# Picks spread over the first PEER product, dots through a ring of three, and POOL making the lower part of U for one quarter in four

## The reference

```python
q = (xb @ w_q).reshape(T, PEER_HEADS, 2, PEER_QDIM // 2)
s = jnp.einsum('thpc,hpkc->thpk', q, sub_keys)
top_s, top_i = lax.top_k(s, PEER_TOPK)
cand = top_s[:, :, 0, :, None] + top_s[:, :, 1, None, :]
best_s, best_c = lax.top_k(cand.reshape(T, PEER_HEADS, PEER_TOPK * PEER_TOPK), PEER_TOPK)
ids = i1 * N_KEYS + i2            # i1, i2 from top_i by best_c
g = jax.nn.softmax(best_s, axis=-1)
act = jax.nn.gelu(jnp.einsum('td,thkd->thk', xb, u_tab[ids]), approximate=False)
w = (g * act).astype(xb.dtype)
out = jnp.einsum('thk,thkd->td', w, v_tab[ids])
```

## Time and profile before

| what | us |
|---|---|
| median of three runs | 2987.31 |
| lowest, highest | 2981.48, 2988.35 |
| the profiled execution's own time | 2983.09 |
| its span | 2981.3 |
| PE busy | 2801.1 (94%) |
| DVE busy | 2345.2 (79%) |
| POOL busy | 1576.7 (53%) |
| ACT busy | 969.3 (33%) |
| first matmul of quarter 0, last quarter's start | 753, 1480.6 |

### The profile page before, as it was taken

How to read it: one execution, slowest core, us unless ns; L and a number is a source line. 1 busy time by engine, 2 the same in 40 slices (tenths; PEclk the granted TensorE clock), 3 DMA queues, 4 the chain that set the end, 5 groups by cost and what they waited for, 6 DMA issues and landing times.

```text
span 2981.3 us, 33747 instructions
## 1 busy us (share of the span) xinstructions
PE 2801.1 (94%) x12016; PEld 2151.1 (72%) x12016; DVE 2345.2 (79%) x3821; ACT 969.3 (33%) x1331; POOL 1576.7 (53%) x1235
## 2 busy tenths in 40 slices
PE   7999689999688899999979999999999999999998
PEld 3546544788567688888767777777777777777776
DVE  2787943587999977777568888888888888888886
ACT  2014232311144466666222323223223223232233
POOL 1999400011011265666157777777777777777640
PEclk9999589999899999999989999999999999999999
DMA  3111010212335599999998888889888888898883
GB/s 121 39 46 54 3 43 0 78 43 78 130 121 170 162 332 366 366 362 362 351 339 304 301 305 317 296 301 317 301 303 310 300 306 308 298 320 288 317 290 142
DMA packets 253976, 685.16 MB, mean 230 GB/s; under 512 B 31984, under 2 KB 97648, under 8 KB 248432
## 3 DMA queue, kind: packets, MB, share of 16 engines
q0 software_dynamic: 104448, 335.81, 32.4%
q1 hardware_dynamic: 83568, 313.65, 28.6%
q10 hardware_dynamic: 65792, 33.56, 3.9%
HBM read 611.60 MB, written 71.30 MB: 229 GB/s over the span
## 4 chain that ended last, share of the span: by engine, by line
PE 66%; DVE 24%; DVEq 3%; issue 2%; DMA 2%; ACT 2%; another core or an unknown queue 1%; SPq 0%; ACTq 0%
PE ps L1604 21%; PE ps L1596 14%; PE ps L1569 11%; PE ps L1527 6%; DVE ps L1214 6%; DVE hnT L895 4%; PE ps L1455 3%; PE ps L1555 3%; PE ps L1364 2%; DVE ul L1187 2%; DVE wl L1284 1%; PE ps L1324 1%; DMA u_raw<-in_uT 1%; DVE lx L1061 1%; PE ps L1419 1%
## 5 line engine op out<-in xcount | busy, mean ns | idle before, releaser
L523 POOL DMA_INDIRECT vring<-in_v_tab,idsA x512 | 547.3, 1069 | 323.9 <-DVE ps L1214 193.9
L1214 DVE SCALAR_TENSOR_TENSOR ps<-vring,hsel,ps 128x1024 f32<-128x1024 f32 x508 | 652.0, 1283 | 15.3 <-DVE ps L1214 0.5
L512 POOL DMA_INDIRECT hsel<-hidden,idsE x384 | 436.8, 1138 | 159.8 <-issue 109.0
L1604 PE MATMUL ps<-vh,wh 128*128 128x512 f32 x1024 | 403.8, 394 | 28.4 <-DVE wl L1284 28.4
L1596 PE MATMUL ps<-xh,uh 128*128 128x512 f32 x1024 | 408.3, 399 | 12.0 <-DVE ul L1187 11.4
L1604 PE MATMUL ps<-vh,wl 128*128 128x512 f32 x1024 | 405.7, 396 | 0.0
L1596 PE MATMUL ps<-xh,ul 128*128 128x512 f32 x1024 | 405.1, 396 | 0.0
L1604 PE MATMUL ps<-vl,wh 128*128 128x512 f32 x1024 | 403.6, 394 | 0.0
L1596 PE MATMUL ps<-xl,uh 128*128 128x512 f32 x1024 | 402.7, 393 | 0.0
L1569 PE MATMUL ps<-hx,xh 128*128 128x512 f32 x768 | 314.5, 410 | 52.9 <-DVE lx L1061 51.6
L498 POOL TENSOR_TENSOR hot<-marks,selG 128x1024 f32<-128x1024 bf16 x64 | 140.1, 2190 | 364.6 <-PE ps L1555 227.0
(11 more groups left out here) (187 smaller groups left out, 4960.7 us busy)
## 6 DMA issues: line engine op xcount, KB each, us to landing
xraw<-in_uX SPq DMA_DIRECT2D x128, 512.0 KB, 6.5
u_raw<-in_uT SPq DMA_DIRECT2D x128, 512.0 KB, 7.3
v_raw<-in_v_tab SPq DMA_DIRECT2D x128, 512.0 KB, 5.4
gates<-gbuf ACTq DMA_DIRECT2D x16, 2048.0 KB, 23.7
gt<-gates SPq DMA_DIRECT2D x32, 1024.0 KB, 7.6
hidden<-hst SPq DMA_DIRECT2D x96, 256.0 KB, 8.1
wqbuf<-in_w_q SPq DMA_DIRECT2D x16, 512.0 KB, 3.4
vring<-in_v_tab,idsA POOLq DMA_INDIRECT x512, 5.8
```

The lines of the kernel that those rows point to most:

```text
L512: nc.gpsimd.indirect_dma_start(out=hsel[:, n, k:k + 1], out_offset=None, in_=hidden_items, in_offset=bass.IndirectOffsetOnAxis(ap=idsE[:, ...
L523: nc.gpsimd.indirect_dma_start(out=vring[r % VS][:, :], out_offset=None, in_=v_rows if r >= P else u_rows, in_offset=bass.IndirectOffsetOn ...
L1214: nc.vector.scalar_tensor_tensor(out=bank2(6), in0=vring[slot][:, :], scalar=w, in1=bank2(6), op0=ALU.mult, op1=ALU.add).then_inc(cb_done, 1)
L1604: last = mm(ps[:, 2 + k % 4, :], w[:, c, tt * P:(tt + 1) * P], v[:, c, dh * 512:(dh + 1) * 512], start=c == 0 and w is wh and v is vh, sto ...
```

## The change

- **Picks.** Five tiles (0, 4, 5, 6, 7; 70 steps) are done by quarter 36; the other three (42 steps) are spread over quarters 36 to 121.
- **Hot blocks** lie at quarters 21 + 1.5 n, the last at 115. The reload of x stays behind block 29.
- **Dots** lie in quarters 41 to 126, in a ring of three buffers (`vring` 2, 4 and 6), with semaphores of their own (`u_got`, `dot_read`); normed x is made at quarter 40. A gather waits for the dot three before. The eight `vring` gathers of V start after the last dot. Other buffers (`cand2`, `best`, `idf` and others) move so that the three are free while picks go on.
- **Lower part of U.** For quarters 6, 10, 14, ... (Q % 4 == 2, 31 of them) POOL makes `lx`, counting `lxp_ready`; DVE makes the others. PE and SP wait for the one or the other.
- **Last block.** Its sums go to `hlast`, not `hst`; SP loads the first gates before the stores of the last block; the reload of rows waits for `hlast`'s stores.
- **exps** (ACT's exponent for a tile) comes one quarter later in ACT's order.

```diff
-PICK_QUARTERS = 44
-X_BLOCK = PICK_QUARTERS // QB - 1
-X_QUARTER = PICK_QUARTERS + 4
+FIRST_PICKS = 1 + HT
+FIRST_QUARTERS = 36
+LAST_PICK = QUARTERS - 6
+X_BLOCK = FIRST_QUARTERS // QB - 1
+X_QUARTER = FIRST_QUARTERS + 4
 DOT_FROM = X_QUARTER + 1
+DOT_SLOTS = (2, 4, 6)
+US = len(DOT_SLOTS)
...
-def picks_done(qb):
-    return min(NT * STEPS_PICK, NT * STEPS_PICK * (qb + 1) // PICK_QUARTERS)
+def picks_done(Q):
+    first = FIRST_PICKS * STEPS_PICK
+    if Q < FIRST_QUARTERS:
+        return first * (Q + 1) // FIRST_QUARTERS
+    return min(NT * STEPS_PICK, first + (NT * STEPS_PICK - first) * (Q + 1 - FIRST_QUARTERS) // (LAST_PICK - FIRST_QUARTERS))
...
+def low_by_pool(Q):
+    return Q >= QB and Q % QB == 2
+
+def lows(Q, pool):
+    return sum(low_by_pool(q) == pool for q in range(Q + 1))
+
+def stores(slot):
+    return len(range(slot, (NB - 1) * PT, HSLOTS))
...
 def hot_quarter(n):
-    return 16 + n * 3 // 2
+    return 21 + n * 3 // 2
...
+def dots_done(Q):
+    return min(P, share(P, QUARTERS - 1 - DOT_FROM, max(0, Q + 1 - DOT_FROM)))
...
+        uring = [vring[k] for k in DOT_SLOTS]
+        hlast = at(0, "hlast", [P, PT, WIDTH])
...
+        def low_done(engine, Q):
+            engine.wait_ge(lxp_ready if low_by_pool(Q) else lx_ready, lows(Q, low_by_pool(Q)))
...
             def load_x(Q):
                 if Q >= QB:
-                    sp.wait_ge(lx_ready, Q - QB + 1)
+                    low_done(sp, Q - QB)
...
                 if B == NB - 1:
                     for c in range(2):
-                        sp.wait_ge(lx_ready, QUARTERS - QB + c + 1)
+                        low_done(sp, QUARTERS - QB + c)
                         sp.dma_start(u_raw[:, c, :], uT[c]).then_inc(u_in[c], 16)
+                    for slot in range(HSLOTS):
+                        sp.wait_ge(hst_out[slot], 16 * stores(slot))
+                    load_gates(0)
                 store_hidden(B)
-                if B == hot_quarter(HT * BLOCKS - 1) // QB + 2:
+                if B == hot_quarter(HT * BLOCKS - 1) // QB + 1:
...
+            def gather_dot(k):
+                if k == 0:
+                    pool.wait_ge(ids_ready, 1)
+                    pool.wait_ge(sel_ready, FIRST_PICKS)
+                elif k >= US:
+                    pool.wait_ge(dot_read, k - US + 1)
+                else:
+                    pool.wait_ge(xt_ready, 1)
+                nc.gpsimd.indirect_dma_start(
+                    out=uring[k % US][:, :], out_offset=None, in_=u_rows,
+                    in_offset=bass.IndirectOffsetOnAxis(ap=idsA[:, 0, k:k + 1], axis=0)).then_inc(u_got[k % US], 16)
...
             for Q in range(QUARTERS):
+                if low_by_pool(Q):
+                    pool.wait_ge(hx_ready, Q + 1)
+                    r = Q % QB
+                    nc.gpsimd.tensor_tensor(lx[r][:, :, :], xraw[:, r, :, :], hx[r][:, :, :].bitcast(F32),
+                                            ALU.subtract).then_inc(lxp_ready, 1)
                 for n in range(HT * BLOCKS):
                     if hot_quarter(n) - 1 == Q:
                         scale_hot(n)
...
+                for k in range(P):
+                    if quarter_of_dot(k) - 2 == Q:
+                        gather_dot(k)
...
-                if e >= HSLOTS:
+                if B < NB - 1 and e >= HSLOTS:
                     act.wait_ge(hst_out[e % HSLOTS], 16 * (e // HSLOTS))
-                nc.scalar.copy(hst[:, e % HSLOTS, :], ps[:, e % HSLOTS, :]).then_inc(h1_free, 1)
+                dst = hlast[:, n, :] if B == NB - 1 else hst[:, e % HSLOTS, :]
+                nc.scalar.copy(dst, ps[:, e % HSLOTS, :]).then_inc(h1_free, 1)
...
-                if Q >= QB:
+                if Q >= QB and not low_by_pool(Q):
                     low_wide(Q)
...
             def hidden_quarter(Q):
                 B, quarter = divmod(Q, QB)
-                pe.wait_ge(lx_ready, Q + 1)
+                low_done(pe, Q)
```

More of the change, by code:

```diff
@@ L126, in hot_quarter, with quarter_of_dot @@
 def hot_quarter(n):
-    return 16 + n * 3 // 2
[L130 to L135, removed]
+    return 21 + n * 3 // 2
+def dots_done(Q):
+    return min(P, share(P, QUARTERS - 1 - DOT_FROM, max(0, Q + 1 - DOT_FROM)))
+def quarter_of_dot(k):
+    return next(Q for Q in range(QUARTERS) if dots_done(Q) > k)
 def row_of_step(step):
@@ L314, in decoder_block @@
         el_in = [sem(f"el_in{k}") for k in range(VALUES_IN)]
-        xt_in, xt_ready, dot_done = sems("xt_in xt_ready dot_done")
+        xt_in, xt_ready, dot_read, dot_done, hlast_out = sems("xt_in xt_ready dot_read dot_done hlast_out")
+        u_got = [sem(f"u_got{k}") for k in range(US)]
         act_ready, wA_ready = sems("act_ready wA_ready")
@@ L380, in store_hidden @@
                     sp.wait_ge(h1_free, e + 1)
-                    sp.dma_start(hidden[n * P:(n + 1) * P, B * WIDTH:(B + 1) * WIDTH],
-                                 hst[:, e % HSLOTS, :]).then_inc(hst_out[e % HSLOTS], 16)
+                    dst = hidden[n * P:(n + 1) * P, B * WIDTH:(B + 1) * WIDTH]
+                    if B == NB - 1:
+                        sp.dma_start(dst, hlast[:, n, :]).then_inc(hlast_out, 16)
+                    else:
+                        sp.dma_start(dst, hst[:, e % HSLOTS, :]).then_inc(hst_out[e % HSLOTS], 16)
             load_wq(0)
@@ L440, in load_group @@
                     sp.dma_start(v_raw[:, c % VR, :], v_tab[g * GC + c]).then_inc(v_in[c], 16)
[L441 to L446, removed]
+                    if c == 1 and not first:
+                        sp.wait_ge(w_ready, g * GC)
                         load_gates(g)
             for c in range(VR):
-                sp.wait_ge(lx_ready, QUARTERS - VR + c + 1)
+                low_done(sp, QUARTERS - VR + c)
             load_group(0, first=True)
@@ L533, in _ @@
                         scale_hot(n)
[L534 to L542, removed]
+                for k in range(P):
+                    if quarter_of_dot(k) - 2 == Q:
+                        gather_dot(k)
+            rows = 0
             values = P
@@ L1202, in combine @@
                     dve.wait_ge(wA_ready, q // PER_GROUP + 1)
[L1203 to L1204 removed]
+                slot = q % VS
+                dve.wait_ge(v_got[slot], 16 * (q // VS + 1))
                 w = hsel[:, n, k:k + 1]
@@ L1222, in normed_rows @@
                 dve.wait_ge(selT_ready, HT)
-                nc.vector.scalar_tensor_tensor(out=bank2(6), in0=vring[6][:, :], scalar=small[:, 40:41], in1=vring[7][:, :],
+                nc.vector.scalar_tensor_tensor(out=bank2(6), in0=uring[1][:, :], scalar=small[:, 40:41], in1=uring[2][:, :],
                                                op0=ALU.mult, op1=ALU.mult).then_inc(xt_ready, 1)
@@ L1254, in _ @@
                     marked += 1
-                for r in range(items_done(Q - 1) if Q else 0, items_done(Q)):
-                    if r < P:
-                        dot(r)
-                    else:
-                        combine(r - P)
+                for k in range(dots_done(Q - 1) if Q else 0, dots_done(Q)):
+                    dot(k)
             for c in range(2):
```

71 lines of the change are left out of this document (37 added, 34 removed).

## The result

| what | us |
|---|---|
| median of the changed kernel, five runs (lowest, highest) | 2967.77 (2964.76, 2973.15) |
| the kernel before beside it on the same chip | 2981.68 (2980.73, 2988.35) |
| ratio, 95% interval | 0.9947 (0.993 to 0.9964) |
| profiled execution's own time, span | 2964.76, 2963.0 |

The change is faster by 14 us. I forecast 45 less: the direction was right, the size three times too large. The time came out nearest to that of the rival of a ring that binds moderately (2963).

What follows compares the result with a forecast made beforehand. DVE with the picks was taken as the bound until they end, then PE. Quarter 127 starting 43 us earlier and 2 us at the turn to the second product, off 2983.1, gave 2938, stated as 2940; range 2922 to 2978.

Steps and rivals of the forecast that it cites:

- the rival of a ring that binds moderately: Dots' ring: a gather of 8.5 us makes a turn of 11.4, quarter 127 starts at 1461, about 2963; chance 0.19.
- The first 36 quarters: Quarters 0 to 36, set by DVE's picks: quarter 36 starts at about 949 us, a gain of 51 us from there.
- Both hold, DVE narrowly: Quarters 36 to 127: DVE needs 4.8 to 5.1 us and POOL 3.8 per quarter of 5.35, both under PE.
- The ring of three: Dots on three buffers: a turn of 10.8 us, gather 7.9 of it; 42.7 turns take 461 us, ending at 1433.
- a dead heat: Dots' ring from quarter 41: a turn of 10.8 us equals PE's own pace of 10.8 us for three dots.
- The eight lows were nearly neutral: First 36 quarters: each lower part of U made by POOL takes 1.2 us from DVE, gives back 0.85 as interference.
- The rival that priced the lows at 2.4 each: POOL's lower parts of U cost DVE 2.4 us each, 12 us more in the first part; about 2960, chance 0.08.
- The last quarter: End of the first product: last gates store taken as 35 us; quarter 127 starts at 1438 against 1480.6, 43 us earlier.
- the turn to the second product: After quarter 127: DVE's 1.48 us wait for gt goes and two loads leave 1 to 2 us earlier, 2 us gained.
- the later counts and not the sum: Start of quarter 127: the store's 1432 lies beside the ring's 1433, so the later sets it, at 1435.
- The ring throughout and slower: Quarters 41 to 126: a gather of 9.6 us makes a turn of 12.5, end 1506, about 3008; chance 0.07.
- The gates store of 53 us: Before quarter 127: the last gates store takes 53 us again, quarter 127 starts at 1450, about 2953; chance 0.11.

## Why the forecast was right, and where it failed

**The first 36 quarters: right in kind, 7 us short.** They gained 36 us, for 44. Quarter 36 starts at 950, for 949, but that match is luck: quarter 0 started 7 us early in this execution, and the stretch took 7 us longer than forecast, 203 for 196. What I had too small is the surplus, 29 us of DVE from quarter 4 to 36, where I had 15.3 for all POOL work. With all lows on DVE the stretch took 198.5 and the surplus was 14.8.

**"Both hold, DVE narrowly" held, but not by relief from POOL.** DVE was busy 398 of 490 us from quarter 41 on, 56 of them surplus (21 before). That is 0.65 us a quarter, inside the 0.5 to 0.8 that I had.

**"The ring of three": this is the step that failed, in two of its terms.** The shares of the two engines were too small. I gave 0.3 + 0.6 for POOL's wake and its own work, and 0.8 for DVE's delay; they measured 1.03 and 1.36. Both together are 0.7 us, nearly all of it DVE's, times 42.7 turns 29 us, and quarter 127 came 30 us after the forecast. I had called it "a dead heat" and then priced it at nothing; in a dead heat every delay is paid. The gather's number was right, 7.85 measured for 7.9, and in part by luck. The 7.9 belongs to 345 GB/s, and the dots' stretch moved 327, for which the two points of the earlier trace rows give 7.0. Traffic alone does not set the time: with two buffers and 265 GB/s a gather took 6.79, and in the second product 5.7 at 303.

**PE's clock had no term.** I took 4.16 us for every quarter. In quarters 36 to 127 PE's granted clock was at the lower of its two levels (1.2 GHz) for 27.3 us, 12.8 in the kernel before and 3.4 in the one without gathers. It fell after idle time of PE each time: from 1452.6 to 1462.8 it was low, with PE idle from 1450.1 until the `lx` at 1456.8, and the 54 matmuls that follow in the chain took 15.51 us where 54 take 12.5. Over the stretch PE was busy 489.8 us for the matmuls that took 477.3 without gathers. So of the 40 us between these two kernels 28 are idle time of PE and 12 are slower matmuls, a consequence of the waits and not a rival to them. No run holds the clock, so how much of the 12 the kernel pays is not shown.

**The eight lows were nearly neutral, as forecast (quarters 0 to 36 took 199.8 us with them alone, 198.5 without); the 23 others had no price.** I costed them at 0.85 us of interference against 1.2 saved, counted both engines' time and found room. What I left out is what stands behind a low in POOL's queue. The low takes 2.4 us there:

```profile
L576 POOL TENSOR_TENSOR lx<-xraw,hx x31: 2357/2408/3381, 761.8 to 1457.6; 128x1024 fp32r<-128x1024 f32 x31
```

The duration came out as forecast from `wql`. But gathers wait behind it, on a ring without slack. With the lows gone from there POOL gets to the issue 0.5 us earlier in a turn (0.55 for 1.03) and DVE to the dot 0.2 earlier, while the gather is 0.3 longer; the turn falls from 11.46 or 11.49 to 11.05 to 11.08, 0.4 x 42.7 = 17 us, of the 20.6 by which quarters 36 to 127 get shorter. And DVE is hardly relieved. By the Trainium skill (Advanced Engine Details and Errata, GPSIMD Details) POOL and DVE share an interface and conflict when DVE has two inputs in SBUF; the traces agree in part: the dots, with one input in PSUM, never grew (58 of them beside work of POOL), but `bdig`, with one input in all, did. In the changed kernel a low took 1.3 us from DVE, and not the whole 2.4; with four buffers it took 2.3. My 0.85 was too little, and the difference made the move worth next to nothing. The rival that priced the lows at 2.4 each came to 2960, near the measured time, but it put the cost on DVE alone and had DVE at 5.5 us of 5.35 a quarter, where DVE was busy 398 of 490 us. PE's own late `lx` from POOL is 9 us at the most, from the run with it one place earlier; the shares overlap and are not added.

So of the missing 30 us, POOL's lows among the gathers account for 21 to 23 by their removal, and the want of a fourth buffer for 9 more (497 to 488, in the time 6). The kernel without both takes 2939.5, which looks like the forecast of 2940, but on a chip where the kernel before took 2978: it is 39 us faster than that, of the 45 forecast. A fourth buffer alone gives 16 of them, since with POOL's lows DVE then nearly binds. Which of the two gets the larger blame depends on which is undone first.

**The last quarter, and the turn to the second product.** I took 35 us for the last gates store, and it took 24.1, and SP waits for it no longer; the 16.3 us wait of the earlier trace rows is gone. It lay beside the ring, and the ring came later, so it gave nothing: "the later counts and not the sum" was right. The load of the gates no longer holds DVE (the earlier trace rows against the first product with the gates, which here has no idle time before it), but the operation ahead of it waits, for an operand of its own:

```profile
1478.83 1.23 DVE L1314 TENSOR_TENSOR vl<-v_raw,vh 128x1024 fp32r<-128x1024 f32 x1 [9.76 <-ACT vh L876]
1479.98 0.69 DVE L1319 TENSOR_TENSOR hg<-hg,gt 128x512 f32<-128x512 f32 x1
```

The 2 us that I counted don't show in the time: 2965.44 with the part undone, 0.9947 of before like the changed kernel. They may be there all the same. On the chips other than the second the stretch from quarter 127 took 1494.6 to 1499.0, 1497 in the mean, in the eleven executions profiled with the part in place, 1499.8 with it undone and 1500.7 before. One execution each of the last two is too little to call it shown.

**The other rivals.** The moderate ring was the right one in its turn (11.4, measured 11.46), but for the wrong reason: it had the excess in the gather (8.5; it was 7.85), and the excess was in the engines' delays. The ring throughout and slower did not come; the run with two buffers shows its mechanism, at 1.0373 of before. The gates store of 53 us did not come either.

**Open.** With four buffers and all lows on DVE `lx` is at 1507 ns in the mean, not 1232. In that kernel 45 of DVE's 123 `lx` of quarters 4 to 126 lay beside a hot scaling of POOL and 22 of them grew; with three buffers it was 14, and 3 grew. So the mean of one operation depends on which operations happen to lie beside POOL's, and the surplus of all is the safer measure. Why they lie together more often with four buffers, and why a low costs DVE 2.3 us then and 1.3 with three, no run takes apart.

## What to carry to other kernels

Before moving work to an engine with time to spare, ask what stands behind it in that engine's queue, and price it there: here each of the 23 operations of 2.4 us beside the gathers, on a half-idle engine, cost the whole kernel about 1 us, in good part through the gathers queued behind it. A ring's pace is the transfer plus the time that both engines take to get to it, and where that equals the consumer's pace leave a buffer of slack, or price every delay; the fourth buffer cost only memory that was free at that time. And check that the relieved engine was relieved, by the time of all its operations in both traces: 19 subtractions fewer in 390 us, and 2 us less in the two largest groups, is no relief.

**The version that beats both:** the changed kernel with four buffers and all lows on DVE, 2939.54 us, 0.9872 (0.9856 to 0.9888) of before, 27 us under the changed kernel beside it.

## What the runs showed of the hardware

- A POOL subtraction of 128x1024 f32 took 1.1 to 1.3 us from DVE's operations around it in three pairs of kernels, in the mean of 31, also when nobody read its result, and 2.3 us in a fourth pair. 31 unused ones made the kernel 26 us slower.
- DVE's operations grew only beside POOL's subtractions and scalings, not beside its issues of gathers (261 of them beside an issue alone, 1 ns in the mean), and dots with one input in PSUM did not grow at all (58 of them beside such an operation).
- POOL's issue of a gather took from 0.94 to 2.01 us: 0.95 in the mean with DVE idle, 1.05 beside dots, 1.66 beside an `lx`.
- Gathers of 128 rows of 4 KB land in 7.85 us with three buffers at 327 GB/s, in 6.79 with two at 265, where I had thought of the gather's time as set by the traffic alone.
- One chip ran the kernel before 110 us slower than another. In the four traces taken there all of it lies behind the first product, and the ratio of the same two kernels stayed the same there (0.9868 and 0.9872).
